# Delta rule gate: Silu applied by ScalarE on the way out of PSUM instead of in place later

## What is computed

```python
def gated_deltanet(x, w_in, conv_w, A_log, dt_bias, onorm_w, w_out):
    proj = x @ w_in
    qkv, z, a, b = jnp.split(proj, [GDN_CONV_CH, GDN_CONV_CH + D_VA, GDN_CONV_CH + D_VA + H], axis=-1)
    qkv = causal_dwconv_silu(qkv, conv_w)
...
    o = chunk_gated_delta_rule(q, k, v, g, beta)
    o = rms_norm(o, onorm_w) * jax.nn.silu(z.reshape(B, L, H, GDN_DV).astype(F32))
    return o.reshape(B, L, D_VA).astype(x.dtype) @ w_out
```

## Time and profile before

| | us |
|---|---|
| median of 3 runs | 2278.31 |
| the 3 runs | 2279.26, 2276.0, 2278.31 |
| span of the profiled execution | 2275.6 |
| TensorE busy | 2094.9 (92%) |
| VectorE busy | 1521.1 (67%) |
| ScalarE busy | 1302.3 (57%) |
| GpSimd busy | 479.4 (21%) |

### The profile page before, as it was taken

The page is one execution under the profiler, slowest core; times in us unless marked ns, Lnnn a source line. Parts: engine busy times, 40 slices in busy tenths (PEclk is TensorE's granted clock), DMA queues, the critical chain, the costliest instruction groups (busy, mean ns, idle before and its releaser), DMA issues. The chain is left out here.

```text
span 2275.6 us, 35281 instructions
## 1 busy us (share of the span) xinstructions
PE 2094.9 (92%) x9793; PEld 1585.0 (70%) x9793; DVE 1521.1 (67%) x2524; ACT 1302.3 (57%) x2160; POOL 479.4 (21%) x367
## 2 busy tenths in 40 slices
PE   7998899898999999999995899998999999999993
PEld 6875799874777767777773755675767677777772
DVE  3762556566788778888774314746877777788884
ACT  3332244532777767777774123532767777778772
POOL 0000355300222222233220300000222222222220
PEclk9999899998999999999997899999999999999996
DMA  6321100016899999999996120125999999999993
GB/s 193 105 75 56 43 20 20 20 56 223 302 369 367 363 338 364 375 367 368 356 357 218 47 70 19 42 96 209 372 336 350 363 348 355 351 371 375 371 353 108
DMA packets 181906, 539.80 MB, mean 237 GB/s; under 512 B 26529, under 2 KB 58177, under 8 KB 181697
## 3 DMA queue, kind: packets, MB, share of 16 engines
q1 hardware_dynamic: 151776, 460.75, 54.1%
q0 software_dynamic: 25248, 69.25, 12.1%
q10 hardware_dynamic: 4800, 8.78, 1.0%
HBM read 504.71 MB, written 54.10 MB: 246 GB/s over the span
## 5 line engine op out<-in xcount | busy, mean ns | idle before, releaser
L1739 DVE TENSOR_TENSOR gu_l<-ring,gu_h 128x1024 fp32r<-128x1024 f32 x512 | 610.6, 1221 | 91.4 <-ACT gu_h L1625 89.3
L1625 ACT CAST gu_h<-ring 128x1024 fp32r<-128x1024 f32 x512 | 523.8, 1060 | 81.8 <-DMA ring<-in_moe_w_up 66.9
L1557 PE MATMUL bank<-gu_h,xgT_l 128*128 128x512 f32 x1024 | 413.9, 404 | 0.0
L1559 PE MATMUL bank<-gu_h,xgT_h 128*128 128x512 f32 x1024 | 402.3, 393 | 0.0
L1558 PE MATMUL bank<-gu_l,xgT_h 128*128 128x512 f32 x1024 | 401.5, 392 | 0.0
L1867 POOL DMA_INDIRECT xg<-h_rows,list_idx x128 | 148.8, 1162 | 907.2 <-issue 456.1
L1596 PE MATMUL bank<-ring,hmT_f 128*128 128x512 f32 x544 | 280.0, 596 | 0.0
L1632 ACT CAST down_h<-ring 128x1024 fp32r<-128x1024 f32 x130 | 136.2, 1047 | 231.2 <-DMA ring<-in_moe_w_down 128.1
L1745 DVE TENSOR_TENSOR down_l<-ring,down_h 128x1024 fp32r<-128x1024 f32 x130 | 159.3, 1226 | 113.8 <-ACT down_h L1632 112.8
L1886 POOL DMA_INDIRECT moe_sum<-y,out_idx x128 | 195.7, 1529 | 172.0 <-issue 146.5
L1559 PEld LDWEIGHTS bank<-gu_h,xgT_h 128*128 128x128 f32 x1024 | 193.6, 189 | 42.7
(11 more groups left out here) (361 smaller groups left out, 3339.9 us busy)
## 6 DMA issues: line engine op xcount, KB each, us to landing
ring<-in_moe_w_gate SPq DMA_DIRECT2D x256, 512.0 KB, 9.7
ring<-in_moe_w_up SPq DMA_DIRECT2D x256, 512.0 KB, 19.4
ring<-in_moe_w_down SPq DMA_DIRECT2D x256, 512.0 KB, 15.9
ring<-in_a_w_in SPq DMA_DIRECT2D x32, 512.0 KB, 5.2
ring<-in_a_w_out SPq DMA_DIRECT2D x8, 512.0 KB, 4.5
h_rows<-ring ACTq DMA_DIRECT2D x8, 512.0 KB, 2.6
moe_sum<-y ACTq DMA_DIRECT2D x8, 512.0 KB, 7.1
ring<-moe_sum SPq DMA_DIRECT2D x8, 512.0 KB, 5.0
```

Of the source, the lines that this page charges most:

```text
L1557: nc.tensor.matmul(out, lhsT=xl, rhs=wh, start=k == 0, stop=False)
L1559: last = nc.tensor.matmul(out, lhsT=xh, rhs=wh, start=False, stop=k == KD - 1)
L1625: nc.scalar.copy(gu_h[:, c, :, :], gate_up_cols(gate_slot, c * CH // 2, CH // 2)).then_inc(gu_hi.sem, 1)
L1739: nc.vector.tensor_tensor(gu_l[:, c, :, :], gate_up_cols(gate_slot, c * CH // 2, CH // 2), gu_h[:, c, :, :].bitcast(F32), ALU.subtract).th ...
```

## The change

In gdn_projections, ScalarE gets the work of VectorE's copy_z: open_gate(half) reads each of the four banks of z as it becomes ready, applies Silu and writes SBUF. The first half's four stand behind act_z_hi(9), the second half's at the end of the casts, ahead of the two Sqrt. copy_z is gone from VectorE. In gdn_delta_rule the four Silu passes in place are gone. VectorE waits once, ahead of the first gate product, for all eight pieces of z.

```diff
@@ gdn_projections, ScalarE
+                def open_gate(half):
+
+                    for tt in range(TT):
+                        act.wait_ge(z_ready.sem, z_ready.base + TT * half + tt + 1)
+                        nc.scalar.activation(z_gate[:, tt, half * 512:(half + 1) * 512], z_bank(half, tt)[:, :], ACT.Silu).then_inc(z_done.sem, 1)
+
...
                     act_z_hi(act, n)
+                    if n == KD + 1:
+                        open_gate(0)
+                open_gate(1)
                 act.wait_ge(sums_copied.sem, sums_copied.base + 2)
                 nc.scalar.activation(k_norm[:, :, :], sum_cols[:, :, H:], ACT.Sqrt)
@@ gdn_projections, VectorE
-                def copy_z(half):
-                    for tt in range(TT):
-                        v.wait_ge(z_ready.sem, z_ready.base + TT * half + tt + 1)
-                        nc.vector.tensor_copy(z_gate[:, tt, half * 512:(half + 1) * 512], z_bank(half, tt)[:, :]).then_inc(z_done.sem, 1)
-
...
                     if n == KD + 1:
-                        copy_z(0)
                         copy_sums()
                     elif n == KD + 3:
                         norms()
-                copy_z(1)
@@ gdn_delta_rule
         def dve_gate(v, tt):
             o = v_tok[:, tt, :, :]
-            v.wait_ge(gate_open.sem, gate_open.base + tt + 1)
+            if tt == 0:
+                v.wait_ge(z_done.sem, z_done.base + 2 * TT)
             nc.vector.tensor_tensor(o, o, heads(z_gate[:, tt, :]), ALU.mult).then_inc(gated_ready.sem, 1)
@@ gdn_delta_rule, ScalarE
-                def open_gate(tt):
-                    nc.scalar.activation(z_gate[:, tt, :], z_gate[:, tt, :], ACT.Silu).then_inc(gate_open.sem, 1)
-
...
-                        elif level > 2 and tt == TT - 1:
-                            open_gate(level - 3)
...
-                        if tt == TT - 1:
-                            open_gate(3)
```

More of the change, by code:

```diff
@@ L764, in build @@
         gated_ready, onorm_in = sem("gated_ready"), sem("onorm_in")
-        rms_in, rms_out, gate_open, gated_hi = after(silu_done, N_QKV), after(side_ready, H), after(squared, 2 * H), after(conv_done, N_QKV)
+        rms_in, rms_out, gated_hi = after(silu_done, N_QKV), after(side_ready, H), after(conv_done, N_QKV)
         def dve_rms_gain(v, tiles):
```

## The result

The kernel became slower by 0.2%. The median is 2282.48 us of 20 runs (2278.62 to 2291.3) against 2277.89 us of 20 runs of the kernel before (2272.51 to 2283.83). The ratio is 1.0023, with a 95% interval of 1.0016 to 1.0030, which is 5.2 us with an interval of 3.6 to 6.8; the two medians are 4.6 us apart. The forecast was 6.1 us and 2284.4 us.

What follows compares the result with a forecast made beforehand. The prediction took TensorE, busy 92% of the span, as the bound. Its terms 1.9 + 1.5 + 1.5 + 1.2 gave +6.1 us, 2284.4 us against the median 2278.3, with a range of 2279.5 to 2287.5 us.

Steps and rivals of the forecast that it cites:

- The last tile, term 0: Last token tile of the delta rule: removing four Silu passes and a table load beside other work gains 0.
- Place one, +1.9: Middle of the gate projection: four Silu ahead of squares 14 and 15 lengthen TensorE's idle from 1.24 to 3.16 us.
- Place two, +1.5: End of the projection stage: table load and two Sqrt queue behind the last Silu, ending at 252.03 instead of 250.49.
- The table load: End of the projection stage: 1.28 us load, next instruction 0.02 us later, without the documented drain of about 1380 ns.
- rival 3: End of the projection stage: a real drain before the table load, at most 1.28 us; +7.4, 2285.7 us; chance 0.08.
- Rival 4: Silu between squares in the gate projection: another table set, two more loads, 2.6 us; +8.7, 2287.0 us; chance 0.03.
- The clock, +1.5 and +1.2: TensorE's clock falls behind both lengthened gaps, mid gate projection and stage end, costing 1.5 and 1.2 us.
- rival 1: TensorE's clock stays up behind both lengthened gaps (+3.4, 2281.7 us) or one (about +4.9, 2283.2 us); chance 0.28.

Runs made afterwards that it cites:

- e4: The kernel before with its four Silu passes in the last token tile left out; ratio 0.9995, -1.1 us against the kernel before.
- e2: The changed kernel with the first half's four Silu put behind squares 14 and 15; ratio 1.0013, +3.0 us against the kernel before.
- e5: The changed kernel with each of the first half's four Silu made twice; ratio 1.0041, +9.3 us against the kernel before.
- e1: The changed kernel with the two Sqrt put ahead of the second half's Silu; ratio 1.0022, +5.0 us against the kernel before.
- e3: The changed kernel with first-half Silu behind squares 14 and 15 and both Sqrt ahead of second-half Silu; ratio 0.9998, -0.5 us against the kernel before.
- e6: The changed kernel with every pair of squares issued one step earlier; ratio 0.9973, -6.1 us against the kernel before.
- e9: The changed kernel run once more, without edits, for a second profile; ratio 1.0019, +4.3 us against the kernel before.
- e8: The kernel before with only every pair of squares issued one step earlier; ratio 0.9963, -8.4 us against the kernel before.
- e11: Repeat of e8, the kernel before with only the squares a step earlier; ratio 0.9971, -6.6 us against the kernel before.

## Why the prediction was right, and which step was not

*The last tile, term 0: no gain, as forecast.* e4 takes the passes away alone and finds nothing outside the noise, and the profile after turns them into idle time. The prediction read TensorE's waits in that tile as 0.2 us where they are 1.9, but none is for ScalarE, so the conclusion held. What the term lacked is a small cost, not a gain: the tile is 0.4 us longer wherever the Silu is moved, for a reason that stays open.

*Place one, +1.9: shown.* Measured 1.98 us between the same instructions, and undone by order alone in e2. The cause is the place in ScalarE's list, not the work: e2 does the same work at no cost. e5 shows the other direction.

*Place two, +1.5: shown.* Measured 1.56 us. e1 and e3 bring the border gap back to 0.9 us. The Exp load of the next stage was moved with it and not doubled, as forecast.

*The table load: the row was right.* In the changed kernel the load starts 0.01 us behind the last Silu and the Sqrt 0.02 us behind the load. The Trainium skill (ScalarE: Activation LUTs, What ACT_TABLE_LOAD costs) states a drain of about 1380 ns beside the load. The trace agrees with its 1283 ns for the load and shows no such drain here, so rival 3 is out. Rival 4 is out as well: no load stands between the first half's Silu and the squares.

*The clock, +1.5 and +1.2: the step that failed.* The prediction took 13 gaps of over 2.1 us, each followed by a fall, and concluded that both new gaps would be followed by one. The price of one fall was right: 1.70 us at place one (e1), 1.58 at place two (e2), though twice that with the longer fall of e6. The certainty was wrong. The gap of 3.18 us was followed by a fall in one of three profiles (e1, and not in the kernel after or e9). That of 2.59 us was followed by one in two of five (e2 and e6, and not in the kernel after, e5 or e9). By these counts the term is 1.70 / 3 plus 2/5 of (1.58 + 3.03) / 2, or 0.6 + 0.9 = 1.5 us, as an estimate from few profiles, in place of 2.7. With it and the last tile the sum is 1.98 + 1.56 + 0.4 + 1.5 = 5.4 us, against 5.2 measured.

What misled was not the kind of gap but the single trace. Among the 13 are gaps like the new ones, with TensorE busy throughout the 4 us before and behind: one of 2.64 us that ends at 812.14, and two of 2.99. Counted in the same way (over 2.1 us, begun at full clock), the other twelve profiles hold 156 such idle stretches, and 25 of them were not followed by a fall within 4 us, where the trace before has none of 13. The same gap in two profiles of one program, once with a fall and once without, rules out length and surroundings as the sole cause; what varies from one execution to the next is left, such as the moment at which the gap comes, and which of it decides was not tried. Nor does 2.1 us bound the falls: in the old trace one followed the gap of 2.07 us that ends at 1896.54 and another the gaps at the start of z, the longer of them 1.87 us.

*How much the good forecast proves.* The time of the kernel can't tell these sums apart: the interval of 3.6 to 6.8 us holds the forecast of 6.1, the 5.4 above, and the 3.9 us without any fall; the 3.4 of rival 1 lies just under it. Both profiles of the kernel after show the clock kept behind both gaps, as in rival 1. That the forecast came within 1 us is therefore partly luck; the terms of places one and two are shown by the rows, and the clock's term is not. In the stated range the two ends are not made alike: 2279.5 is 2.2 us under 2281.7, and 2287.5 is 1.8 over 2285.7.

*The profile's own span.* Its 7.1 us looked like a bigger effect than forecast. The stages touched account for 2.35 of it (276.92 - 274.57), and 4.26 came in the next stage, with a lower clock than the second profile of the same kernel has there.

## What to carry to other kernels

An engine with 43% idle time can still be the wrong home for 2 us of work, if its list has one place where the bound engine waits for it. Before moving work to it, look for the instruction behind the new one and ask who waits for that: here the squares, which TensorE wanted at once, and a Sqrt whose table load had been free. Putting the awaited work first cost nothing and undid the loss (e3), and applied to every step of the kernel before it brought 8.4 and 6.6 us (e8, e11), while for the change itself no gain was shown.

## What the runs showed of the hardware

The same idle gap of TensorE, of the same length and between the same instructions, is followed by its lower clock in one profile and not in another, even of the same program (3.18 us: one of three profiles; 2.59 us: two of five; the 2.99 us near the end: eight of thirteen), and a fall behind the first two cost 1.6 to 3.0 us. So single profiles of kernels that differ by such a gap can differ by several microseconds in stages that nobody touched, and the stage times must be compared piece by piece. A switch of ScalarE's table cost the 1.28 us of the load and 0.01 to 0.02 us around it.
